# Attention's set-up apart from its loop, expert rows added into the residual by scatter, and group sums copied out of PSUM by ScalarE

## Time and profile before

| | |
|---|---|
| runs | 2191.21, 2191.83, 2192.27 us; median 2191.83 |
| the profiled execution | 2191.35 us, span 2189.6 us, mean granted clock 0.926 |
| project | 0 to 445.4 us |
| attend | to 1198.3 us |
| mix | to 1478.4 us |
| route | to 1500.1 us |
| experts | 1501.9 to 2096.2 us |
| combine | to 2189.6 us |

### The profile page before, as it was taken

The page is one execution under the profiler, slowest core; times in us unless marked ns, Lnnn a source line. Parts: engine busy times, 40 slices in busy tenths (PEclk is TensorE's granted clock), DMA queues, the critical chain, the costliest instruction groups (busy, mean ns, idle before and its releaser), DMA issues. The chain is left out here.

```text
span 2189.6 us, 26611 instructions
## 1 busy us (share of the span) xinstructions
PE 1880.3 (86%) x8674; PEld 1448.1 (66%) x8674; DVE 1234.1 (56%) x1938; ACT 702.4 (32%) x1091; POOL 641.9 (29%) x662
## 2 busy tenths in 40 slices
PE   2999999937999999999997699992999999999900
PEld 2677878814656656656655488882998899998800
DVE  5667576555775775776775644435333343333359
ACT  2435343202333333333333233220223322223234
POOL 5677776601211211211211311100232333323100
PEclk9999999966999999999999699996999999999955
DMA  7555656300000000000000444424788887888478
GB/s 288 178 158 169 183 143 173 106 33 1 8 8 5 7 7 5 7 7 5 7 7 27 157 160 147 150 96 145 247 270 273 277 278 270 278 265 274 164 300 332
DMA packets 214685, 307.54 MB, mean 140 GB/s; under 512 B 22901, under 2 KB 166480, under 8 KB 212314
## 3 DMA queue, kind: packets, MB, share of 16 engines
q1 hardware_dynamic: 191002, 228.99, 32.3%
q0 software_dynamic: 18944, 69.21, 8.7%
q10 hardware_dynamic: 4672, 8.56, 1.0%
HBM read 245.91 MB, written 60.82 MB: 140 GB/s over the span
## 5 line engine op out<-in xcount | busy, mean ns | idle before, releaser
L823 PE MATMUL tbank<-KR,VV 128*128 128x512 f32 (+3 forms) x640 | 299.3, 549 | 27.2 <-DVE on L919 27.2
L1015 ACT ACTIVATE KR<-tbank 128x512 f32<-128x512 f32 (+1 forms) x320 | 170.3, 532 | 334.1 <-PE tbank L800 330.9
L903 DVE TENSOR_REDUCE cmax<-tbank 128x1 f32<-128x512 f32 (+2 forms) x340 | 205.8, 607 | 76.9 <-PE tbank L761 67.5
L1038 POOL TENSOR_SCALAR diag<-cst,nmax 128x128 fp32r<-128x128 f32 x138 | 84.1, 610 | 533.4 <-DVE nmax L906 533.4
L798 PE MATMUL tbank<-Qhi,Khi 97*128 97x512 f32 (+2 forms) x321 | 216.9, 676 | 0.0
L348 PE MATMUL pbank<-hhi,wslhi 128*128 128x512 f32 x512 | 205.5, 401 | 4.5 <-DVE wsllo L399 2.8
L1724 DVE TENSOR_SCALAR xTe<-ebank,modcol 128x256 f32<-128x256 f32 (+1 forms) x128 | 53.7, 472 | 260.4 <-PE ebank L1644 139.2
L348 PE MATMUL pbank<-hhi,wsllo 128*128 128x512 f32 x512 | 200.0, 391 | 0.0
L348 PE MATMUL pbank<-hlo,wslhi 128*128 128x512 f32 x512 | 199.6, 390 | 0.0
L1666 PE MATMUL ebank<-xTe,wg 128*128 128x192 f32 x1024 | 171.8, 326 | 3.1 <-DVE ahi L1752 1.8
L1666 PEld LDWEIGHTS ebank<-xTe,wg 128*128 128x128 f32 x1024 | 167.9, 190 | 7.8 <-DVE aT L1748 2.1
(11 more groups left out here) (261 smaller groups left out, 3517.7 us busy)
## 6 DMA issues: line engine op xcount, KB each, us to landing
wg<-in_w_exp_gate SPq DMA_DIRECT2D x32, 1024.0 KB, 5.9
wu<-in_w_exp_up SPq DMA_DIRECT2D x32, 1024.0 KB, 10.2
wd<-in_w_exp_down SPq DMA_DIRECT2D x32, 1024.0 KB, 7.7
wraw<-in_w_in SPq DMA_DIRECT2D x60, 512.0 KB, 3.8
wmod<-in_w_ada POOLq DMA_DIRECT2D x16, 1024.0 KB, 7.0
y<-y_dram SPq DMA_DIRECT2D x16, 1024.0 KB, 21.3
wada<-in_w_ada SPq DMA_DIRECT2D x2, 4096.0 KB, 22.5
xt<-in_x SPq DMA_DIRECT2D x4, 2048.0 KB, 12.4
```

Of the source, the lines that this page charges most:

```text
L823: ins = pe.matmul(out, VV[:, kt, 2 * b:2 * b + 2].rearrange("p c d -> p (c d)"), step_of(probs, m), start=kt == 0, stop=last)
L903: W(ve.tensor_reduce(cmax[:, i % 2, n:n + 1], plain[:, chunk % 2, 0:w], AX.X, ALU.max), plain_read)
L1015: A(act.activation(step_of(probs, m), scores[:, m % 2, j * P:512], ACT.Exp), exp_done)
```

## The change

- **project**: `LATE` is 32, so a piece has 128 columns and `wmod` is half as large. In the room that becomes free, with some tiles now sharing storage (`xsq` with `hf`, `uc` with `sq1`, `t4` with `conv`), the attention weights are loaded in project (six loads on SyncE's queue) and scaled by VectorE at group 2, slice 14. ScalarE and VectorE get some waits for the shared tiles.
- **attend, set-up**: four key products and four query products go each to a PSUM bank of its own. The value parts use banks as they come free. ScalarE copies rotary and mask rows that VectorE copied; GpSimd fills zeros and ones. The second head's rows come behind the first head's. Exponentials get a tile `probs` of their own.
- **attend, loop**: behind the first exponential of each group ScalarE copies the finished group's bank to `raw` in SBUF (`copy_out`), which gives the bank free. VectorE divides from `raw` at the steps of `DIVIDE_AT`.
- **route and experts**: the gates go into the marks as three bf16 parts, so a slot has six numbers. VectorE copies both results out of PSUM times gate times g2 (`out_first`, `out_rest`). The scatters add into `x2_dram` (`compute_op=ALU.add`), four per pair of experts, and each waits until the earlier ones have landed.
- **combine**: reads x2 alone, 8 loads of two tiles, and normalizes. `y_dram` is gone.

The core of the diff, in the order of the stages (indentation cut by eight columns):

```diff
-LATE = 16
+LATE = 32
 LATE_W = 4 * D // LATE
...
+    q = T["w_uq"].rearrange("l (k p) n -> p (l k) n", p=P)
+    sp.dma_start(wuq[:, :, 0:HEADS * QKD], q).then_inc(ld_up, 16)
+    sp.dma_start(wuq[:, :, HEADS * QKD:], q[:, :, 0:QKD]).then_inc(ld_up, 16)
+    for w, name, more in ((wuk, "w_uk", 1), (wuv, "w_uv", 2)):
+        src = T[name].rearrange("l p n -> p (l n)")
+        sp.dma_start(w[:, 0:HEADS * NOPE], src).then_inc(ld_up, 16)
+        sp.dma_start(w[:, HEADS * NOPE:], src[:, 0:more * NOPE]).then_inc(ld_up, 16)
...
+            if (n, s) == (2, 14):
+                ve.wait_ge(ld_up, 16 * 6)
+                for k in range(KQ):
+                    V(ve.tensor_scalar(wuq[:, k], wuq[:, k], cols[:, R_Q + k:R_Q + k + 1], SM, ALU.mult, ALU.mult))
+                V(ve.tensor_scalar(wuk[:], wuk[:], cols[:, R_KV:R_KV + 1], None, ALU.mult))
+                V(ve.tensor_scalar(wuv[:], wuv[:], cols[:, R_KV:R_KV + 1], None, ALU.mult))
...
+            if n:
+                act.wait_ge(lo_done, n * KD)
...
+DIVIDE_AT = {m: (g, r) for g, steps in ((GROUPS - 1, (6, 7, 8, 10)), (0, (12, 13, 14, 16)),
+                                (1, (18, 19, 20, 22)), (2, (28, 29, 30, 31)))
+     for r, m in enumerate(steps)}
...
-probs = KR
+probs = sb("probs", [P, 4 * 512])
...
+raw = sb("raw", [P, 2, 512])
...
-                sp.wait_ge(out_free, hp * 2 * GROUPS + (b * GROUPS + g + 2))
+                sp.wait_ge(divided, hp * 2 * GROUPS + (b * GROUPS + g + 4))
...
-    for c in range(8):
-        if c:
-            pe.wait_ge(made_dve, c)
-        make(c, 0)
+    for n in range(4):
+        pe.matmul(bank[0:NOPE, n], wk[:, 0], kvn[:, n * 512:(n + 1) * 512], start=True, stop=True
+                  ).then_inc(made_done, 1)
+    for n in range(4):
+        for k in range(KQ):
+            ins = pe.matmul(bank[:, 4 + n], wq[:, 0, k], qn[:, k, n * 512:(n + 1) * 512],
+                            start=k == 0, stop=k == KQ - 1)
+        ins.then_inc(made_done, 1)
+    for v in range(V_EARLY):
+        pe.wait_ge(made_dve, V_EARLY_AFTER[v])
+        make_values(v, 0, bank[:, V_EARLY_BANK[v]])
...
     pe.wait_ge(qlo_done, 4)
+    pe.wait_ge(rope_ready, 1)
...
+    pe.wait_ge(rows_act, 8)
+    pe.wait_ge(rows_pool, 2)
+    pe.wait_ge(rope_rest, 1)
+    pe.wait_ge(filled, 2)
+    pe.wait_ge(v_copied, V_EARLY)
...
+        W(ve.reciprocal(rs[:, r * P:(r + 1) * P], raw[VD:P, g % 2, r * P:(r + 1) * P]))
         if r == 3:
             p = (g + 1) % 2
             ve.wait_ge(stored[p], (head * 2 + (g + 1) // 2) * 16)
             W.wait()
-            W(ve.tensor_tensor(on[:, p], outp[0:VD, g % 2], rs[:], ALU.mult), out_free)
...
+            W(ve.tensor_tensor(on[:, p], raw[0:VD, g % 2], rs[:], ALU.mult), divided)
...
+    weights(0, 0)
+    W(ve.tensor_copy(onesr[:], cst[:, C_ONE:C_ONE + P]))
+    for n in range(4):
+        at = slice(n * 512, (n + 1) * 512)
+        ve.wait_ge(khi_done, n + 1)
+        W(ve.tensor_tensor(Klo[0:NOPE, 0, at], bank[0:NOPE, n], Khi[0:NOPE, 0, at].bitcast(F32),
+                           ALU.subtract), made_dve)
...
+        ve.wait_ge(qlo_done, max(n - 1, 0))
+        W.wait()
+        W(ve.tensor_tensor(qf[0:QKD, n % 2], bank[0:QKD, 4 + n], cs[0:QKD, at], ALU.mult))
+        W(ve.tensor_tensor(turned_q[NOPE:QKD], bank[QKD:P, 4 + n], cs[QKD:P, at], ALU.mult), made_dve)
+        W.wait()
+        W(ve.tensor_tensor(qf[NOPE:QKD, n % 2], qf[NOPE:QKD, n % 2], turned_q[NOPE:QKD], ALU.add),
+          qf_ready)
...
+    W(ve.memset(outp[:, 1], 1.0), out_set)
...
+    def rope_low(b):
+        ve.wait_ge(rope_ready, b + 1)
+        W(ve.tensor_tensor(Klo[NOPE:QKD, b], KR[NOPE:QKD], Khi[NOPE:QKD, b].bitcast(F32), ALU.subtract), rope_rest)
+    rope_low(0)
...
-                if kt < 4:
-                    if g:
-                        divide(kt, g - 1, hp * 2 + b)
-                    else:
-                        divide(kt, GROUPS - 1, hp * 2 + (b - 1))
+                if m in DIVIDE_AT:
+                    d, r = DIVIDE_AT[m]
+                    divide(r, d, hp * 2 + (b - 1 if d == GROUPS - 1 else b))
...
+    def copy_out(g, head):
+        act.wait_ge(out_done, head * GROUPS + (g + 2))
+        act.wait_ge(divided, head * GROUPS + (g + 2))
+        A(act.activation(raw[:, g % 2], outp[:, g % 2], ACT.Copy), out_free)
...
+    def rope(b):
+        A(act.activation(Khi[NOPE:QKD, b], KR[NOPE:QKD], ACT.Copy), rope_ready)
...
+    def mask_rows(b, g):
+        for k, parts in enumerate((Khi, Qhi)):
+            A(act.activation(parts[below, b, g * 512:(g + 1) * 512], qf[below, k], ACT.Copy), rows_act)
...
+    rope(0)
...
+        act.wait_ge(made_done, n + 1)
+        A(act.activation(Khi[0:NOPE, 0, at], bank[0:NOPE, n], ACT.Copy), khi_done)
...
+    for n in range(4):
+        part(2 * n + 1, 0, 0)
+        if n < V_EARLY:
+            copy_values(n, 0, bank[:, V_EARLY_BANK[n]])
+        mask_rows(0, n)
+    rope(1)
...
+                if kt == 0:
+                    copy_out((g - 1) % GROUPS, hp * 2 + (b if g else b - 1))
...
+    zero = cst[QKD:QKD + 1, C_ID:C_ID + 1].to_broadcast([1, S])
+    for b in range(2):
+        for k, lows in enumerate((Klo, Qlo)):
+            po.tensor_scalar(lows[QKD:QKD + 1, b], zero, 0.0, None, ALU.mult).then_inc(rows_pool, 1)
+            po.wait_ge(rows_pool, 2 * b + k + 1)
+        if b == 0:
+            for k in (1, 3):
+                po.memset(VV[:, :, k], 1.0).then_inc(filled, 1)
+                po.wait_ge(filled, k // 2 + 1)
+            for n in range(4):
+                rest(n, 0, 0)
...
+    for i, left in enumerate((gates, gleft[:, 0], gleft[:, 1])):
+        do(ve.tensor_copy(gpart[:, i], left if i else gates[:]))
+        if i < 2:
+            do(ve.tensor_tensor(gleft[:, i], left if i else gates[:], gpart[:, i], ALU.subtract))
+        for k in range(2):
+            do(ve.tensor_tensor(marks[:, :, k, (3 + i) * NEXP:(4 + i) * NEXP], pick[:, :, k],
+                                across(gpart[:, i, k::2].unsqueeze(2), NT, NEXP), ALU.mult))
...
-        po.indirect_dma_start(out=y_dram, in_=y, in_offset=None,
+        po.indirect_dma_start(out=x2_dram, in_=y, in_offset=None, compute_op=ALU.add,
...
         hold(po, st_ya[b], r * (PAIRS * 16) + q * 16, passed_pool)
+        hold(po, st_yb[b], r * (PAIRS * 16) + q * 16, passed_pool)
         po.tensor_copy(ja[:, b:b + 1], dest_a[:, bass.ds(r * 0 + q * 2 + b, 1)]).then_inc(dest_copied, 1)
-        hold(po, dest_copied, r * (PAIRS * 3) + q * 3 + (b + 1), passed_pool)
+        po.tensor_copy(jb[:, b:b + 1], dest_b[:, bass.ds(r * 0 + q * 2 + b, 1)]).then_inc(dest_copied, 1)
+        hold(po, dest_copied, r * (NEXP * 2) + q * 4 + (b * 2 + 2), passed_pool)
...
+        hold(po, st_ya[1 - b], r * (PAIRS * 16) + q * 16 + b * 16, passed_pool)
+        hold(po, st_yb[1 - b], r * (PAIRS * 16) + q * 16 + b * 16, passed_pool)
         hold(po, ya_done, r * NEXP + q * 2 + (b + 2), passed_pool)
         put(ya[:, b], ja[:, b:b + 1], st_ya[b])
...
-    def scatter_b(q, r):
...
+        hold(po, yb_done, r * NEXP + q * 2 + (b + 2), passed_pool)
+        put(yb[:, b], jb[:, b:b + 1], st_yb[b])
...
-        for out, lo, n in ((bank[:, 4, 0:3 * NEXP], 0, P), (bank[0:CAPB, 5, 0:3 * NEXP], P, CAPB),
...
+        for out, lo, n in ((bank[:, 4, 0:MARKS * NEXP], 0, P), (bank[0:CAPB, 5, 0:MARKS * NEXP], P, CAPB),
...
+        ve.scalar_tensor_tensor(yb[:, b], outb.rearrange("p a n -> p (a n)"),
+                                gate_b[:, bass.ds(r * 0 + q * 2 + b, 1)], g2row[0:CAPB], ALU.mult, ALU.mult
+                                ).then_inc(yb_done, 1)
...
+    def out_first(q, b, r):
+        ve.wait_ge(down_a, r * NEXP + q * 2 + (b + 1))
+        ve.wait_ge(st_ya[b], r * (PAIRS * 16) + q * 16)
+        ve.scalar_tensor_tensor(ya[:, b], outa.rearrange("p a n -> p (a n)"),
+                                gate_a[:, bass.ds(r * 0 + q * 2 + b, 1)], g2row[:], ALU.mult, ALU.mult
+                                ).then_inc(ya_done, 1)
...
+x2, res = sb("x2f", [P, NT, D]), sb("res", [P, NR, D])
...
+    for i in range(NL):
+        sp.dma_start(x2[:, 2 * i:2 * i + 2], x2_dram[2 * i * P:(2 * i + 2) * P, :].rearrange(
+            "(q p) d -> p q d", p=P)).then_inc(ld[i], 16)
...
+        sp.dma_start(out_rows[t * P:(t + 1) * P, :], res[:, t % NR]).then_inc(st_out[t % NR], 16)
...
-        hold(act, ld[t % NB], 32 * (t // NB + 1), passed)
-        act.activation(y[:, t % NB, 0], y[:, t % NB, 0], ACT.Copy, scale=gates[:, 2 * t:2 * t + 1]
-                       ).then_inc(first_gated, 1)
...
-        ve.scalar_tensor_tensor(res[:, t % NR], x2[:, t % NB], stat[:, t % NB, 2:3], fgrow[:],
-                                ALU.mult, ALU.mult).then_inc(normed, 1)
...
-        ve.scalar_tensor_tensor(y[:, b, 1], y[:, b, 1], gates[:, 2 * t + 1:2 * t + 2], y[:, b, 0],
-                                ALU.mult, ALU.add).then_inc(summed, 1)
...
-        ve.tensor_tensor(y[:, b, 0], y[:, b, 1], g2row[:], ALU.mult).then_inc(gated, 1)
```

(69 more changed lines are left out.)

233 lines of the change are left out of this document (95 added, 138 removed).

## The result

The changed kernel takes 2219.45 us (median of 4 runs, 2215.54 to 2222.69), before 2191.52 in the same comparison: 27.9 us slower, ratio 1.0124, 95% interval 1.0109 to 1.0139. The forecast was slower by 14, at 2205 in a range of 2172 to 2250. The sign and the range hold; the size of the move is twice the forecast.

A forecast was written before the change was run, and what follows sets the result against it. A stage costs what its last engine costs, and GpSimd becomes project's last. Terms 119-31-44+0.7+9.4+0+7-47 = +14 give 2205 us, range 2172 to 2250.

The forecast's parts named there:

- The stage ends then and not at 445: +119: Project: GpSimd's 32 pieces, 18.6 us each and 14.2 once others are idle, end at 564, +119 us.
- The rest of project's edits ... have those 119 us to hide behind and cost 0: Project: six more loads, four scalings and waits for shared tiles cost 0; without cover up to 5 us.
- Set-up, "-31": Attend up to the first score: from 81.1 us to 49 to 50, -31 (-22 to -41).
- Loop, "-44": Attend's loop: TensorE's 27.2 us of waits for the division go, plus 17.5 of lost clock, less 1: -44.
- Route and table, "+9.4": Route and table: products before the ranks 5.3, the table's 96 wider products +3.8, VectorE's longer chain +0.6: +9.4 us.
- Experts, "0", and the drain, "+7": Experts: VectorE's copies and adding scatters cost 0; at the end the last two scatters land one after the other, +7 us.
- Combine, "-47": Combine: from 93.4 us to 46, bound by transfers at 423 GB/s, -47 (-43 to -52).
- (2): Project: GpSimd's pieces shrink nearly in proportion, project ends below 551, so the kernel is faster, 2161 us; chance 0.25.
- (3): Experts: scatter landings above 14 us set the pace, +100 us, so 2305; chance 0.06.
- (4): Border of project and attend: stages don't meet, set-up runs beside GpSimd's last pieces, -20, 2185 us; chance 0.04.
- (5): Attend's loop: ScalarE waits for TensorE's last value product, TensorE runs dry 0.6 us 32 times, +20, 2225; chance 0.08.
- The estimate from the Trainium skill's lock rule: Project: hindrance goes by number of instructions, 4.3 a piece, 19.4 us a piece, end 10 us later, sum near 2215.

The follow-up runs named there:

- LATE alone: The kernel before with LATE = 32 and nothing else; 2313.99 us against 2188.98, ratio 1.0562.
- the run with tiles held: The kernel before with LATE = 32, shared tiles and their waits, and the attention weights' tiles held unused through project; 2307.45 us.
- experiment 3: The changed kernel with 16 pieces of 256 columns, each loaded in four quarters into two buffers in turn; 2085.25 us, ratio 0.9516.
- Experiment 5: The changed kernel with the four rows of zeros written by ScalarE and not by GpSimd; 2206.55 us against the changed kernel's 2219.45.

## Why the prediction was right or wrong

- **"The stage ends then and not at 445: +119"**: the mechanism is right and for its own edit the size is too (+120 with LATE alone). The terms: instructions undisturbed 8.0 (forecast 8.1); hindrance 2.9 with LATE alone and 3.2 in the changed kernel (3.5); the load's wait 4.3 and 4.8 (3.9), 3.6 when all else is idle (2.9). The first two errors cancelled the third, with LATE alone.
- **"The rest of project's edits ... have those 119 us to hide behind and cost 0"** is the step that failed. They hide from VectorE, TensorE and SyncE, but not from GpSimd, which had become the one that sets the end. Whatever hinders its instructions or loads is then paid in full: one piece less by 445 us, 14 to 15 us more. A cover of 119 us is none for what acts on the engine that makes it. In the last 70 us before 443 VectorE's subtractions fall on GpSimd's scalar products (877 ns and not 640) and a load is waited for 1.8 us longer than in the run with tiles held. Taking the scalings out gives 3 to 9 us back; by which way, and why the load's wait grew, stays open. With quarters (experiment 3), where GpSimd is done at 418, the whole amount is gone.
- **Set-up, "-31"**: measured -25.5. The two rows ahead of the diagonals were priced right (5.4 each, forecast 5.3). Left out were the two at the start: GpSimd's first row holds VectorE's weight copies, 5.4 us before the first product. Left out too was that VectorE holds up the last low half of the queries, 1.9 us. Experiment 5 took GpSimd's rows away, and set-up fell by 13.
- **Loop, "-44"**: measured -44.8 with the tail, -45 when made alone. The 17.5 us for the clock, read from one stretch and a mean, held: TensorE's busy time fell by 19.
- **Route and table, "+9.4"**: +9.1; the 96 products took 9.83 us where 9.5 was worked out.
- **Experts, "0", and the drain, "+7"**: TensorE stays at 140.00 of 140, the drain is +3.8, of which the add is 2. The Trainium skill's rule on an adding DMA (page "Collectives: The Full Stack", section "The bandwidth ceiling: the fold count and why AG ≠ RS ≠ AR") gave an estimate of a share toward 0.95: 0.93 with the add, 0.82 without. The direction is borne out; the landing rose from 6.7 and 7.3 to 8.3, not to double.
- **Combine, "-47"**: -48.7, at 410 GB/s.
- **The rivals**: project's end at 580 is far from the 551 below which (2) would have decided, and where GpSimd keeps up the kernel gains 104 us (experiment 3), on the side that (2) supposed. Scatters land in 8.3 and not above 14 (3). All engines start attend within 0.1 us of each other at 580.6, after 3 us of waiting for GpSimd's last store (4). The loop's new wait is 0.9 us, once (5).
- **Hindrance**: with 256 columns it was 4.3 us a piece, with 128 it is 2.9 to 3.2. Times the pieces of the first 445 us that is nearly one sum: 4.3x16 = 69, 2.9x24 = 70, 3.2x23 = 74. So it goes rather by what VectorE does in the stage, the same in all three, than by the number or the width of GpSimd's instructions; in the changed kernel 42 of 73 us lie in instructions that met one of VectorE's 64 subtractions of 128x1024. (With quarters it is 3.5x16 = 56, by 418 us.)
- **The estimate from the Trainium skill's lock rule**, 4.3 a piece, was too high for this, and it was added up wrongly: at 19.4 a piece 22.5 pieces are done by 443 us, 9.5x14.2 = 135 more end at 578, 14 us later than 564 and not 10, and the sum is 2219 and not 2215. That this lies so near the measured 580.6 and 2219.45 is luck, since the hindrance it rests on was not there and longer waits for loads stood in its place. The rule itself is seen at attend's start (below).
